# Gated heads taken in pairs, with the four values of a pair projected token-major

## The chip, the cores and the metric

The kernel runs on one core of a Trainium2 chip. The metric is the device time of one execution in microseconds (us); lower is better. The engines are named as the profile names them: PE is TensorE (PEld its weight loads), DVE is VectorE, ACT is ScalarE, POOL is GpSimd and SP is SyncE.

## The reference, cut to what matters

Two transformer blocks of 512 tokens and width 1024 are computed in float32. The change lies in the first block, where eight heads run side by side. Each head has an mLSTM part (a) and a stick-breaking part (b), and their sum is gated:

```python
p = rms_norm(x, norm_mix_g) @ w_in        # q_a k_a v_a o_a i_a f_a q_b k_b v_b g_a g_b
qk_a = silu(causal_conv(concat(q_a, k_a), conv_w))
h_a = mlstm_chunkwise(q_a, k_a, v_a, i_pre, f_pre)          # P @ v_a over s <= t, 64 wide keys, 128 wide values
y_a = sigmoid(o_a) * head_rms_norm(h_a)
y_b = stick_breaking(head_rms_norm(q_b), head_rms_norm(k_b), v_b)   # A @ v_b over s < t, 128 wide
y = sigmoid(g_a + b) * y_a + sigmoid(g_b + b) * y_b
x = x + y @ w_out
```

After it come the MLP of the first block (1024 to 4096 and back) and the second block, which the change leaves as they are.

## The kernel before, in words

**Projections.** Every projection is made of tiles of 128 output rows by 512 columns. A tile is eight steps over the width of 1024, and in each step three matmuls in the single-pass float32 format (high part by high part, low by high, high by low), 24 in all (`project`, L294). The result goes into one of two PSUM banks of `proj`, by the parity of the tile's number; a tile waits until the tile before the last has been read out (`tile_free`). Four tiles share a weight group of 2 MB. A group comes from HBM in two halves (`w_raw`, a queue on SP), ACT makes its high half (`split_hi`, L261), DVE its low half (`split_lo`, L267), and there are two slots for split groups. With `tokens=True` the activations are the stationary operand and the weights stream, so that the tile comes out with tokens on the partitions; otherwise features are on the partitions.

**A head.** Head `h` has eight tiles: 0 q_b, 1 k_b, 2 q_a and k_a together, 3 v_b (first group), 4 v_a, 5 o_a, 6 g_a, 7 g_b (second group). All are feature-major. Attention needs the values token-major, so ACT copies tiles 3 and 4 out of PSUM into `v_bT` and `v_aT`, PE turns them by eight 128x128 transposes (L1439), and ACT copies the turned ones back into `v_b` and `v_a` (L583, L584). The other small steps of a head on PE are the sums of squares of q_b and k_b (L1424, L1425), the stick scores (L1430), the gated scores (L1446), ten transposes of the stick weights `beta` (L1456), the gated sums with `decay` as the stationary operand and `v_a` streaming (L1462), four transposes of `y_tok` (L1468), and the stick sums with `v_b` (L1411).

**The order of the work is written out by hand for each engine,** with semaphores between them. On PE a head is: tiles 0, 1, 2, squares, tile 3, stick scores, tiles 4, 5, value transposes, gated scores, tile 6, `beta` transposes, gated sums, tile 7, `y_tok` transposes, stick sums; then the next head begins. So while one of the slower chains on ACT, DVE and POOL runs, PE makes a projection tile. Three such chains matter here:

- gated weights: ACT's exponential of `decay` (L581), DVE's product with the gated scores (L1000), POOL's causal mask (L449), and then the gated sums on PE;
- token norm: after the gated sums four squares on ACT (L592), small steps on DVE (L1007 to L1013), a logarithm and an exponential on ACT (L595, L597), DVE's product into `y_tok` (L1015), and then the `y_tok` transposes on PE;
- end of a head: after the stick sums five steps on DVE (L1028 to L1035), the last of which sets `head_done`. ACT's copies of the next head, POOL's broadcast of the next head's row of gates (`bc`, L439) and the output projection wait for it.

ACT has two table sets in use: one with logarithm and exponential, one with the sigmoid. A change of set is one ACT_TABLE_LOAD, four in each head. Head 0 is written out and heads 1 to 7 are a loop. The output projection (`G_OUT`, eight tiles, the last step of the first of which waits for the last `head_done`) follows at once.

Of the kernel before, what the change touches and what calls it, by code (L numbers as in the profile page):

```python
# [9 lines left out]
ALU = mybir.AluOpType  # L10
# [3 lines left out]
P = 128  # L14
# [8 lines left out]
DQK_A = 64  # L23
HD_B = 128
# [53 lines left out]
def program(nc, x_in, wall, gains, head_par, sb_gains, b_if, *rest):  # L78
    *block2_in, out = rest
    with ExitStack() as ctx:  # L80
# [41 lines left out]
        def at(name, offset, shape, dt=F32):  # L122
# [13 lines left out]
        names = "q_b k_b sq_q sq_k conv silu k_a v_bT v_aT v_b gate_o gate_a gate_b".split()  # L136
        (q_b, k_b, sq_q, sq_k, conv, silu, k_a, v_bT, v_aT, v_b, gate_o, gate_a, gate_b) = [
            at(n, (61 + 2 * i) * K, [P, SEQ]) for i, n in enumerate(names)]
        v_a = at("v_a", 87 * K, [P, TB, P + 1])
        y_tok, scl = sq_k, silu  # L140
# [272 lines left out]
        def _(pool):  # L413
# [11 lines left out]
            gp.memset(v_a[:, :, P:P + 1], 1.0).then_inc(S["consts"], 1)  # L425
# [73 lines left out]
        def _(act):  # L499
# [39 lines left out]
            with a.Fori(0, HEADS) as h:  # L539
                n = T_HEADS + 8 * h  # L540
                ga = G_HEADS + 2 * h

                a.preload_act_table_set("natural_log_exp_and_others")
                split_hi(ga + 1, 0, 0)

                for j, (raw, sq) in enumerate(((q_b, sq_q), (k_b, sq_k))):
                    a.wait_ge(S["tile_made"], n + j + 1)
                    a.wait_ge(S["head_done"], h + 1)
                    a.activation(raw[:, :], proj[:, j], ACT.Copy)
                    a.activation(sq_hi[:, j], proj[:, j], ACT.Square)  # L550
                    a.activation(sq[:, :], proj[:, j], ACT.Square).then_inc(S["tile_free"], 1)
                split_hi(ga + 1, 0, 1)

                a.wait_ge(S["tile_made"], n + 3)
# [9 lines left out]
                a.wait_ge(S["tile_made"], n + 4)  # L564
                a.activation(v_bT[:, :], proj[:, 1], ACT.Copy).then_inc(S["tile_free"], 1)
                split_hi(ga + 2, 1, 0)
# [5 lines left out]
                a.wait_ge(S["tile_made"], n + 5)  # L572
                a.activation(v_aT[:, :], proj[:, 0], ACT.Copy).then_inc(S["tile_free"], 1)

                a.activation(silu[:, :], conv[:, :], ACT.Sigmoid).then_inc(S["silu_sig"], 1)
                a.preload_act_table_set("natural_log_exp_and_others")
                split_hi(ga + 2, 1, 1)
                a.wait_ge(S["tile_made"], n + 6)
                a.activation(gate_o[:, :], proj[:, 1], ACT.Copy).then_inc(S["tile_free"], 1)
                a.wait_ge(S["arg_a"], 4 * h + 4)  # L580
                a.activation(decay[:, :], decay[:, :], ACT.Exp).then_inc(S["decay_exp"], 1)  # L581
                a.wait_ge(S["v_turned"], h + 1)
                a.activation(v_b[:, :], pa[:, 0:512], ACT.Copy).then_inc(S["v_sb"], 1)  # L583
                a.activation(v_a[:, :, 0:P], pa[:, 512:1024].rearrange("p (t n) -> p t n", t=TB), ACT.Copy).then_inc(S["v_sb"], 1)  # L584
                a.wait_ge(S["tile_made"], n + 7)
                a.activation(gate_a[:, :], proj[:, 0], ACT.Copy).then_inc(S["tile_free"], 1)
                a.wait_ge(S["a_turned_b"], h + 1)
                a.activation(aT[:, :], pa[:, 0:TRI_COLS], ACT.Copy).then_inc(S["a_b"], 1)

                a.wait_ge(S["num_made"], h + 1)  # L590
# [8 lines left out]
                a.wait_ge(S["tile_free"], n + 7)  # L599
                a.activation(gate_o[:, :], gate_o[:, :], ACT.Sigmoid).then_inc(S["gate_sig"], 1)  # L600
                a.activation(gate_a[:, :], gate_a[:, :], ACT.Sigmoid, bias=par[:, 5:6]).then_inc(S["gate_sig"], 1)
                a.wait_ge(S["tile_made"], n + 8)
                a.activation(gate_b[:, :], proj[:, 1], ACT.Sigmoid, bias=par[:, 6:7]).then_inc(S["tile_free"], 1)
# [297 lines left out]
        def _(dve):  # L901
# [4 lines left out]
            v.memset(tick[:, 2:3], 0.0).then_inc(S["pad_zero"], 1)  # L906
            def square_sum(t):
# [42 lines left out]
            with v.Fori(0, HEADS) as h:  # L950
                ga = G_HEADS + 2 * h

                v.wait_ge(S["head_done"], h + 1)
# [4 lines left out]
                split_lo(ga + 1, 0, 0)  # L958
                for j, sq in enumerate((sq_q, sq_k)):
                    v.wait_ge(S["tile_free"], T_HEADS + 8 * h + j + 1)  # L960
                    v.tensor_tensor(sq_lo[:, j], sq[:, :], sq_hi[:, j], ALU.subtract).then_inc(S["sq_lo"], 1)
                split_lo(ga + 1, 0, 1)
# [5 lines left out]
                v.wait_ge(S["par_head"], 3 * h + 3)  # L968
                v.wait_ge(S["pad_zero"], h + 2)
                v.wait_ge(S["tile_free"], T_HEADS + 8 * h + 3)  # L970
# [5 lines left out]
                split_lo(ga + 2, 1, 0)  # L976

                v.wait_ge(S["bc_landed"], 16 * h + 16)
                for i in range(TB):
                    v.tensor_scalar(decay[:, TRI[i]:TRI[i] + SEQ - P * i], bc[:, P * i:], col[:, i:i + 1], 0.0,  # L980
                                    ALU.add, ALU.min).then_inc(S["arg_a"], 1)
                v.wait_ge(S["silu_sig"], h + 1)
# [3 lines left out]
                v.tensor_copy(k_a[DQK_A:P, :], silu[0:DQK_A, :]).then_inc(S["silu_done"], 1)  # L986
                v.wait_ge(S["keep_masked"], 4 * h + 4)
# [9 lines left out]
                split_lo(ga + 2, 1, 1)  # L997
# [4 lines left out]

                v.wait_ge(S["num_sq"], 4 * h + 4)
                for i, (sign, least) in enumerate(((-1.0, floor[:, :]), (1.0, tok[:, 0]))):
# [13 lines left out]

                v.wait_ge(S["y_turned"], h + 1)
                v.wait_ge(S["gate_sig"], 2 * h + 1)  # L1020
                v.scalar_tensor_tensor(scl[:, :], pm[:, 1024:1536], par[:, 4:5], gate_o[:, :], ALU.mult, ALU.mult)\
                    .then_inc(S["y"], 1)
                v.wait_ge(S["gate_sig"], 2 * h + 2)
                v.wait_ge(S["y"], 4 * h + 1)
                v.tensor_tensor(scl[:, :], scl[:, :], gate_a[:, :], ALU.mult).then_inc(S["y"], 1)
                v.wait_ge(S["pv_b_made"], h + 1)
                v.wait_ge(S["tile_free"], T_HEADS + 8 * h + 8)
                v.tensor_tensor(gate_b[:, :], pa[:, 0:512], gate_b[:, :], ALU.mult).then_inc(S["y"], 1)  # L1028
                v.wait_ge(S["y"], 4 * h + 3)
                v.tensor_tensor(scl[:, :], scl[:, :], gate_b[:, :], ALU.add).then_inc(S["y"], 1)  # L1030
                v.wait_ge(S["y"], 4 * h + 4)
# [4 lines left out]
                    .then_inc(S["head_done"], 1)  # L1036
            v.wait_ge(S["head_done"], HEADS + 1)
# [334 lines left out]
        def _(pe):  # L1372
# [12 lines left out]
            def gate_rows():  # L1385
# [7 lines left out]
                mm.then_inc(S["a_turned"], 1)  # L1393

            def head(h, first=False):
                n = T_HEADS + 8 * h
                ga = G_HEADS + 2 * h

                def tile(j):
# [383 lines left out]
```

## Time and profile before

| | us |
|---|---|
| median of 3 runs | 1264.02 (1262.86 to 1264.53) |
| the profiled execution | 1262.79 |
| its span, first to last instruction | 1260.5 |
| PE busy in the span | 1240.2 (98%) |
| DVE busy | 694.1 (55%) |
| ACT busy | 606.6 (48%) |
| POOL busy | 47.8 (4%) |

A row of a timeline gives the start of an instruction from the start of the span, its duration, engine, line, operation, what it writes and reads, and how many neighbours were merged into it; in brackets stands how long the engine had been idle before it and what released it. Matmuls are pipelined: each lasts longer than the distance to the next, so what a matmul costs is the distance of the starts. PEclk is the clock granted to TensorE, 1.00 being 2.4 GHz.

### The profile page before, as it was taken

What the parts mean: (1) busy time and instruction counts of PE and PEld (TensorE: products, weight loads), DVE (VectorE), ACT (ScalarE), POOL (GpSimd) and SP (SyncE); (2) the same over time, 40 slices, a digit from 0 to 9 for tenths busy, and PEclk for the clock granted to TensorE, in tenths of its full rate; (3) what the DMA queues carried; (4) which work ended last, traced back from release to release, by engine and by line L of the source; (5) the groups of instructions that cost most, each with busy time, mean ns of one, the idle gap of its engine ahead of it and who ended that gap; (6) DMA issues with size and microseconds to landing.
All of it is one profiled execution on the core that took longest, in us unless ns stands there. A gap on an engine that the chain in (4) does not pass through costs nothing.

```text
span 1260.5 us, 15952 instructions
## 1 busy us (share of the span) xinstructions
PE 1240.2 (98%) x5912; PEld 1008.2 (80%) x5912; DVE 694.1 (55%) x1179; ACT 606.6 (48%) x894; POOL 47.8 (4%) x146
## 2 busy tenths in 40 slices
PE   6999999999999999999999999999999999999998
PEld 5788888888888888888888888888867777677787
DVE  6646455554645555552443433445468989666671
ACT  6745565564556563441321421335456655566820
POOL 1000000000000020000000000000000000000000
PEclk9999999999999999999999999999999999999999
DMA  6323222132322234223231322333213233535621
GB/s 219 110 75 100 75 67 87 64 100 75 100 75 67 85 125 168 68 88 113 68 132 67 100 100 100 101 108 150 76 67 110 104 119 129 201 126 166 251 67 67
DMA packets 26398, 134.48 MB, mean 107 GB/s; under 512 B 3224, under 2 KB 4312, under 8 KB 13552
## 3 DMA queue, kind: packets, MB, share of 16 engines
q1 hardware_dynamic: 16992, 107.49, 25.3%
q0 software_dynamic: 4752, 16.92, 3.9%
q10 hardware_dynamic: 4608, 9.44, 2.0%
q8 instruction: 32, 0.52, 0.2%
q14 instruction: 14, 0.11, 0.0%
HBM read 122.28 MB, written 11.55 MB: 106 GB/s over the span
## 4 chain that ended last, share of the span: by engine, by line
PE 84%; DVE 10%; ACT 3%; issue 2%; DMA 1%; ACTq 0%; DVEq 0%; SPq 0%
PE proj L294 74%; DVE idx L1271 2%; DVE w_lo L267 2%; DVE top L1267 2%; PE pm L1462 1%; PE pa L1411 1%; PE pa L1430 1%; DVE p_sb L1250 1%; PE pm L1446 1%; PE pa L1648 1%; ACT w_hi L261 1%; PE pa L1456 1%; ACT p_sb L792 1%; DVE p_sb L1261 1%; DVE idx L1164 1%
## 5 line engine op out<-in xcount | busy, mean ns | idle before, releaser
L294 PE MATMUL proj<-h_hi,w_hi 128*128 128x512 f32 (+1 forms) x976 | 385.7, 395 | 2.0 <-DVE w_lo L267 1.0
L294 PE MATMUL proj<-h_hi,w_lo 128*128 128x512 f32 (+1 forms) x976 | 377.1, 386 | 0.0
L294 PE MATMUL proj<-h_lo,w_hi 128*128 128x512 f32 (+1 forms) x976 | 376.7, 386 | 0.0
L267 DVE TENSOR_TENSOR w_lo<-w_raw,w_hi 128x2048 fp32r<-128x2048 f32 x100 | 227.9, 2290 | 89.8 <-ACT w_hi L261 88.9
L261 ACT ACTIVATE w_hi<-w_raw 128x2048 fp32r<-128x2048 f32 x100 | 189.8, 1912 | 127.0 <-PE proj L294 121.3
L294 PEld LDWEIGHTS proj<-h_hi,w_hi 128*128 128x128 f32 x976 | 183.4, 188 | 46.0 <-issue 9.9
L294 PEld LDWEIGHTS proj<-h_lo,w_hi 128*128 128x128 f32 x976 | 183.5, 188 | 38.3 <-issue 2.9
L294 PEld LDWEIGHTS proj<-h_hi,w_lo 128*128 128x128 f32 x976 | 183.3, 188 | 37.5
L294 PE MATMUL proj<-w_hi,act_hi 128*128 128x512 f32 x256 | 99.8, 390 | 0.0
L294 PE MATMUL proj<-w_lo,act_hi 128*128 128x512 f32 x256 | 99.6, 389 | 0.0
L294 PE MATMUL proj<-w_hi,act_lo 128*128 128x512 f32 x256 | 99.6, 389 | 0.0
L1097 DVE TENSOR_TENSOR x_res<-x_res,proj 128x512 f32<-128x512 f32 x32 | 21.9, 686 | 92.2 <-PE proj L294 92.2
L633 ACT ACTIVATE relu<-proj 128x512 f32<-128x512 f32 x32 | 19.2, 599 | 106.5 <-PE proj L294 106.5
L1083 DVE TENSOR_TENSOR relu_sq<-relu 128x512 f32<-128x512 f32 x32 | 22.2, 694 | 73.4 <-ACT relu L633 73.4
L294 PE MATMUL proj<-w_hi,h_hi 128*128 128x512 f32 (+1 forms) x160 | 62.2, 389 | 0.0
L294 PE MATMUL proj<-w_lo,h_hi 128*128 128x512 f32 (+1 forms) x160 | 61.9, 387 | 0.0
L294 PE MATMUL proj<-w_hi,h_lo 128*128 128x512 f32 (+1 forms) x160 | 61.7, 386 | 0.0
L294 PEld LDWEIGHTS proj<-w_hi,act_lo 128*128 128x128 f32 x256 | 48.1, 188 | 10.0
L294 PEld LDWEIGHTS proj<-w_lo,act_hi 128*128 128x128 f32 x256 | 48.1, 188 | 10.0
L294 PEld LDWEIGHTS proj<-w_hi,act_hi 128*128 128x128 f32 x256 | 48.1, 188 | 9.8
L792 ACT ACTIVATE p_sb<-p_sb,mx 128x128 f32<-128x128 f32 (+1 forms) x64 | 35.1, 550 | 31.8 <-DVE mx L1253 31.8
L294 PEld LDWEIGHTS proj<-w_hi,h_hi 128*128 128x128 f32 x160 | 30.0, 188 | 7.4 <-issue 1.5
(394 smaller groups left out, 1650.2 us busy)
## 6 DMA issues: line engine op xcount, KB each, us to landing
w_raw<-in_wall SPq DMA_DIRECT2D x100, 1024.0 KB, 5.1
gates<-gate_st ACTq DMA_DIRECT2D x24, 256.0 KB, 2.1
m_all<-gates POOLq DMA_DIRECT2D x2, 1280.0 KB, 7.5
x_res<-in_x ACTq DMA_DIRECT2D x4, 512.0 KB, 5.2
bc<-gate_rows POOLq DMA_DIRECT2D x8, 256.0 KB, 3.5
x_res<-in_x POOLq DMA_DIRECT2D x4, 512.0 KB, 4.8
x<-x_res POOLq DMA_DIRECT2D x1, 2048.0 KB, 7.4
g_all<-gates POOLq DMA_DIRECT2D x1, 2048.0 KB, 11.2
```

Source lines behind the costliest of these rows:

```text
L261: nc.scalar.activation(w_hi[:, slot, 4 * half:4 * half + 4, :], w_raw[:, half], ACT.Copy)\
L267: nc.vector.tensor_tensor(w_lo[:, slot, 4 * half:4 * half + 4, :], w_raw[:, half], w_hi[:, slot, 4 * half:4 * half + 4, :], ALU.subtract)\
L294: mm = nc.tensor.matmul(proj[:, bank, 0:cols] if tokens else proj[:, bank, toks], lhsT, rhs, start=(k == 0 and q == 0), stop=(k == kts - 1 ...
L633: a.activation(relu[:, i % 2], proj[:, i % 2], ACT.Relu).then_inc(S["tile_free"], 1)
L792: a.activation(x, x, ACT.Exp, bias=mx[:, u, i:i + 1], accum_out=row_sum[:, u, i:i + 1])\
L1083: v.tensor_tensor(relu_sq[:, i % 2], relu[:, i % 2], relu[:, i % 2], ALU.mult).then_inc(S["a_sq"], 1)
L1097: v.tensor_tensor(xx, xx, proj[:, t % 2], ALU.add).then_inc(S["tile_free"], 1)
L1164: v.scalar_tensor_tensor(idx[:, c], rel[h % 2][:, c], w_idx[:, i, h:h + 1], idx[:, c] if h else causal[:, 384 - P * i:512], ALU.mult, ALU. ...
L1250: v.tensor_tensor_reduce(p_sb[u][:, c], X[:, c], mask(i), scale(i), -3.0e38, ALU.add, ALU.max, mx[:, u, i:i + 1]).then_inc(S[f"smax{u}"], 1)
L1261: v.tensor_scalar(x, x, row_sum[:, u, i:i + 1], None, ALU.mult).then_inc(S[f"p_norm{u}"], 1)
L1267: v.max(top8[:, i - 1, :], idx[:, LOW[i]:LOW[i] + P * (i + 1)]).then_inc(S["top_max"], 1)
L1271: v.match_replace(x, top8[:, i - 1, :], x, TAKEN).then_inc(S["top_out"], 1)
```

## The change

Two heads `h = 2p` and `2p + 1` make a pair, with four weight groups and sixteen tiles: 0 q_b, 1 k_b, 2 q_a k_a, 3 o_a of the even head; 4 to 7 the values; 8 g_a and 9 g_b of the even head; 10 q_b, 11 k_b, 12 q_a k_a, 13 o_a, 14 g_a, 15 g_b of the odd head. The value group holds v_b and v_a of both heads side by side (512 columns), and its four tiles are token-major, one for each block of 128 tokens. ACT copies each of them straight into `v_b` and `v_a`, which now have room for two heads. The eight value transposes and the two buffers between are gone. The number of tiles, 64, stays.

```diff
+PAIRS = HEADS // 2
+QKA, O_A, VALUES, G_A, G_B, NEXT = (2, 12), (3, 13), 4, (8, 14), (9, 15), 16
...
+            def value_tile(n, t):
+                a.wait_ge(S["tile_made"], n + VALUES + t + 1)
+                a.activation(v_b[:, :, t], proj[:, t % 2, 0:2 * P].rearrange("p (u d) -> p u d", u=2), ACT.Copy)
+                a.activation(v_a[:, :, t, 0:P], proj[:, t % 2, 2 * P:4 * P].rearrange("p (u d) -> p u d", u=2), ACT.Copy)\
+                    .then_inc(S["tile_free"], 1)
...
-                t_.wait_ge(S["tile_free"], n + 5)
-                t_.wait_ge(S["z_sb"], 2 * h + 2)
-                for m, vT in enumerate((v_bT, v_aT)):
-                    for i in range(TB):
-                        mm = t_.transpose(pa[:, 512 * m + P * i:512 * m + P * (i + 1)], vT[:, P * i:P * (i + 1)], ident[:, :])
-                mm.then_inc(S["v_turned"], 1)
```

The order on PE for a pair; tiles 16 and 17 are q_b and k_b of the next pair and are made ahead of it. The last pair, written out after a loop over the other three, has none:

```diff
+            def pair(p, more=True):
+                n_v = T_HEADS + 16 * p + VALUES
+                for u in range(2):
+                    h = 2 * p + u
+                    if u:
+                        for j in (9, 10, 11):
+                            head_tile(p, j)
+                    head_tile(p, QKA[u])
+                    square_sums(h)
+                    head_tile(p, O_A[u])
+                    stick_scores(h)
+                    head_tile(p, G_A[1] if u else VALUES)
+                    head_tile(p, G_B[1] if u else VALUES + 1)
+                    gated_scores(h)
+                    if u == 0:
+                        head_tile(p, VALUES + 2)
+                        head_tile(p, VALUES + 3)
+                    elif more:
+                        head_tile(p, NEXT)
+                    stick_turns(h)
+                    gated_sums(h, u, n_v)
+                    if u == 0:
+                        head_tile(p, G_A[0])
+                    elif more:
+                        head_tile(p, NEXT + 1)
+                    head_turns(h, u)
+
+            head_tile(0, 0, first=True)
+            head_tile(0, 1)
+            gate_rows()
+            with t_.Fori(0, PAIRS - 1) as p:
+                pair(p)
+            pair(PAIRS - 1, more=False)
```

`gated_sums` waits for its masked weights (`p_masked`) as before and, new, for the last value tile to be read out:

```diff
+            def gated_sums(h, u, n_v):
                 t_.wait_ge(S["p_masked"], 4 * h + 4)
+                t_.wait_ge(S["tile_free"], n_v + TB)
```

On ACT the gates are no longer copied out and passed through the sigmoid later: the sigmoid reads the tile in PSUM (`gate_tile`). The order of ACT in the odd head:

```diff
+                h = 2 * p + 1
+                a.preload_act_table_set("natural_log_exp_and_others")
+                for j in range(2):
+                    qk_tile(n + 10 + j, 2 * p + 1, j)
+                conv_tile(h, n + QKA[1])
+                gate_tile(n + O_A[1], gate_o)
+                split_hi(g + 4, 1, 0)
+                sticks(h)
+                split_hi(g + 4, 1, 1)
+                a.wait_ge(S["par_head"], 3 * h + 3)
+                gate_tile(n + G_A[1], gate_a, par[:, 5:6])
+                gate_tile(n + G_B[1], gate_b, par[:, 6:7])
+                a.preload_act_table_set("natural_log_exp_and_others")
+                decays(h)
+                if more:
+                    split_hi(g + 5, 0, 0)
+                    qk_tile(n + NEXT, 2 * p + 2, 0)
+                stick_turns(h)
+                variance(h)
+                if more:
+                    qk_tile(n + NEXT + 1, 2 * p + 2, 1)
+                    split_hi(g + 5, 0, 1)
```

and in the even head: `conv_tile`, `gate_tile` of tile 3, a `split_hi`, `sticks`, value tile 0, the preload of the other table set, a `split_hi`, value tile 1, `decays`, value tiles 2 and 3, `stick_turns`, `variance`, a `split_hi`, `gate_tile` of tile 8, a `split_hi`, `gate_tile` of tile 9. DVE has the steps of before in a like order; its product of the stick sums with `gate_b` counts up `pv_read`, and the sums of squares on PE now wait for that and no more for `head_done`. `y_tok` has a place of its own and no longer shares that of `sq_k`. The columns of the weight groups are laid out on the host to match.

## Rows read from the trace of the kernel before

**Rows 1.** The page: engines, granted clock by slice, one costly group of DVE.
```profile
PE 1240.2 (98%) x5912; PEld 1008.2 (80%) x5912; DVE 694.1 (55%) x1179; ACT 606.6 (48%) x894; POOL 47.8 (4%) x146
...
PEclk9999999999999999999999999999999999999999
...
L267 DVE TENSOR_TENSOR w_lo<-w_raw,w_hi 128x2048 fp32r<-128x2048 f32 x100 | 227.9, 2290 | 89.8 <-ACT w_hi L261 88.9
```

**Rows 2.** Two stretches: length; busy (instructions) of PE, PEld, DVE, ACT, POOL; clock; DMA.
```profile
35.35:466.32 430.97, 430.97 (x2048) 351.04 (x2049) 228.15 (x315) 243.65 (x341) 29.13 (x105) 1.00 0.26 85
471.87:488.19 16.32, 16.32 (x73) 13.51 (x72) 6.76 (x15) 1.56 (x3) 0.57 (x2) 1.00 0.55 196
```

**Rows 3.** Timeline of PE in the third head, first instruction of each step.
```profile
134.96 0.47 PE L294 MATMUL proj<-h_hi,w_hi 128*128 128x512 f32 x1
...
157.74 0.27 PE L1430 MATMUL pa<-k_b,q_b 128*128 128x128 f32 x1
...
159.49 0.80 PE L294 MATMUL proj<-h_hi,w_hi 128*128 128x512 f32 x1
...
165.38 0.39 PE L294 MATMUL proj<-h_hi,w_hi 128*128 128x512 f32 x1
...
170.83 0.27 PE L1439 MATMUL pa<-ident,v_bT 128*128 128x128 f32 x1
...
171.79 0.69 PE L1446 MATMUL pm<-silu,k_a 64*128 64x512 f32 x1
...
173.28 0.50 PE L294 MATMUL proj<-h_hi,w_hi 128*128 128x512 f32 x1
...
178.88 1.25 PE L1456 MATMUL pa<-ident,beta 128*128 128x128 f32 x10
179.97 0.28 PE L1462 MATMUL pm<-v_a,decay 128*128 128x129 f32 x1
...
182.12 0.48 PE L294 MATMUL proj<-h_hi,w_hi 128*128 128x512 f32 x1
...
187.68 0.60 PE L1468 MATMUL pm<-ident,sq_k 128*128 128x128 f32 x4
...
190.19 0.47 PE L294 MATMUL proj<-h_hi,w_hi 128*128 128x512 f32 x1
```

**Rows 4.** Timeline of ACT in the same head.
```profile
171.52 1.26 ACT L581 ACTIVATE decay<-decay 128x1280 f32<-128x1280 f32 x1
...
179.07 0.60 ACT L586 ACTIVATE gate_a<-proj 128x512 f32<-128x512 f32 x1 [5.32 <-PE proj L294]
...
187.88 0.69 ACT L603 ACTIVATE gate_b<-proj,par 128x512 f32<-128x512 f32 x1 [0.51 <-PE proj L294]
188.58 1.28 ACT L543 ACT_TABLE_LOAD   x1
```

**Rows 5.** Timeline of DVE in the same head.
```profile
154.70 0.75 DVE L965 SCALAR_TENSOR_TENSOR k_b<-k_b,sbg,sq_k 128x512 f32<-128x512 f32 x1 [0.49 <-ACT sq_k L563]
...
175.05 1.49 DVE L1000 SCALAR_TENSOR_TENSOR decay<-pm,decay 128x1280 f32<-128x1280 f32 x1
...
184.84 0.69 DVE L1015 TENSOR_TENSOR sq_k<-pm,tok 128x512 f32<-128x512 f32 x1 [0.51 <-ACT tok L597]
...
192.67 0.69 DVE L1035 TENSOR_TENSOR y_lo<-silu,y_hi 128x512 f32 x1
```

**Rows 6.** Timeline of POOL in the same head.
```profile
176.60 1.03 POOL L449 TENSOR_SCALAR_AFFINE_SELECT decay<-decay 128x128 f32<-128x128 f32 x4 [10.39 <-DVE decay L1000]
```

**Rows 7.** Timeline of ACT in the second block: a tile read out in two halves.
```profile
892.08 0.38 ACT L694 ACTIVATE kv_b<-proj 128x256 f32<-128x256 f32 x1 [3.36 <-PE proj L294]
892.36 0.38 ACT L695 ACTIVATE t_k<-proj 128x256 f32<-128x256 f32 x1
```

**Rows 8.** Timeline of PE at the start: three transposes early, and three later.
```profile
8.51 0.84 PE L336 MATMUL pa<-ident,xs 128*128 128x128 f32 x3
...
13.40 0.49 PE L336 MATMUL pa<-ident,xs 128*128 128x128 f32 x3
```

More of the change, by code:

```diff
@@ L135, in program @@
         bc = at("bc", 57 * K, [P, SEQ])
[L136 to L140, printed above, removed]
+        q_b, k_b, sq_q, sq_k, conv, silu, k_a = [
+            at(n, (61 + 2 * i) * K, [P, SEQ]) for i, n in enumerate("q_b k_b sq_q sq_k conv silu k_a".split())]
+        v_b = at("v_b", 75 * K, [P, 2, TB, P])
+        gate_o, gate_a, gate_b = [at(n, (79 + 2 * i) * K, [P, SEQ]) for i, n in enumerate(("gate_o", "gate_a", "gate_b"))]
+        v_a = at("v_a", 85 * K, [P, 2, TB, P + 1])
+        y_tok, scl = at("y_tok", 59 * K, [P, SEQ]), silu
         qk_pad = at("qk_pad", 47 * K, [P, 3 + SEQ])
@@ L538, in _, with qk_tile, conv_tile @@
             a.activation(g_out[:, 1, :], g_m[:, :], ACT.Exp, scale=-1.0).then_inc(S["rows_act"], 1)
[L539 to L554, printed above, removed]
+            def qk_tile(n, heads, j):
+                raw, sq = ((q_b, sq_q), (k_b, sq_k))[j]
+                a.wait_ge(S["tile_made"], n + 1)
+                if heads is not None:
+                    a.wait_ge(S["z_made"], heads)
+                a.activation(raw[:, :], proj[:, j], ACT.Copy)
+                a.activation(sq_hi[:, j], proj[:, j], ACT.Square)
+                a.activation(sq[:, :], proj[:, j], ACT.Square).then_inc(S["tile_free"], 1)
+            def conv_tile(h, n):
+                a.wait_ge(S["tile_made"], n + 1)
                 a.wait_ge(S["head_done"], h + 1)
@@ L1393, in gate_rows, with head_tile, square_sums @@
                 mm.then_inc(S["a_turned"], 1)
[L1395 to L1399, printed above, removed]
[L1400 to L1421 removed]
+            def head_tile(p, j, first=False):
+                made(project(G_HEADS + 4 * p + j // 4, (1 + j // 4) % 2, T_HEADS + 16 * p + j, j % 2, j % 4, first=first,
+                             tokens=VALUES <= j < VALUES + TB))
+            def square_sums(h):
+                t_.wait_ge(S["pv_read"], h + 1)
                 for j in range(2):
@@ L1470, in head, with pair @@
                 t_.wait_ge(S["a_b"], h + 1)
-                weighted(pa[:, 0:512], lambda i: v_b[:, P * i:P * (i + 1)], aT).then_inc(S["pv_b_made"], 1)
-            head(0, first=True)
-            with t_.Fori(1, HEADS) as h:
-                head(h)
+                for i in range(TB):
+                    mm = t_.matmul(pa[:, P * i:SEQ], v_b[:, u, i], aT[:, TRI[i]:TRI[i] + SEQ - P * i],
+                                   start=(i == 0), stop=(i == TB - 1))
+                mm.then_inc(S["pv_b_made"], 1)
+            def pair(p, more=True):
+                n_v = T_HEADS + 16 * p + VALUES
[10 more added lines that the diff above has]
+                    head_tile(p, G_B[1] if u else VALUES + 1)
+                    gated_scores(h)
+                    if u == 0:
[3 more added lines that the diff above has]
+                        head_tile(p, NEXT)
+                    stick_turns(h)
+                    gated_sums(h, u, n_v)
[8 more added lines that the diff above has]
+            with t_.Fori(0, PAIRS - 1) as p:
+                pair(p)
+            pair(PAIRS - 1, more=False)
             t_.wait_ge(S["head_done"], HEADS)
```

192 lines of the change are left out of this document (122 added, 70 removed).

## The prediction

> **What bounds the kernel now.** I read the page first: PE is busy for 98% of the span and the granted clock stands at its upper level, 2.4 GHz, in every slice [rows 1]. Then the window over the heads: from the third tile of head 0 to the first output tile it is 430.97 us, and PE is busy in all of them, DVE in 228 and ACT in 244 [rows 2]. So here only what PE issues sets the time, and every chain of the other engines is covered by a projection tile. The timeline of one head shows the cost of each step as the distance of the starts [rows 3]: a head is 190.19 - 134.96 = 55.23 us; a tile is 165.38 to 170.83 = 5.45; after the stick scores 5.89, after the gated scores 5.60, after the gated sums 5.56, since a float32 step still drains there.
>
> **What is removed.** Eight transposes a head, 170.83 to 171.79 = 0.96 us, with the switch to the next step in them [rows 3]; eight heads make 7.7 us. From below: ten `beta` transposes take 1.09, 0.109 each, so eight alone are 0.87, or 7.0 in all [rows 3]. I take 7.7, as the gated scores will now follow a tile, and the `beta` transposes do so at no visible switch. (The Trainium skill, "TensorE: Matmul & The Clock Gate", part on PE-mode transpose, puts a 128x128 transpose at about 275 ns within a kernel; 64 of them would be an estimated 17.6 us. The rows differ: one lasts 0.27 but the next starts 0.11 later, and the start counts.)
>
> **What is turned round.** The value tiles stream weights over stationary activations instead of the reverse. The output tiles do just that: three of them fill 16.32 us, 5.44 each [rows 2]. Cost zero; it is 64 tiles before and after.
>
> **What leaves ACT.** Two copies into `v_bT` and `v_aT`, two back, and the copies of two gates a head; value tiles cost two copies of 256 columns, a pattern that shows as 0.28 from first start to second and 0.38 for the second, 0.66 for the tile [rows 7]. Table loads go from eight to six a pair. ACT was busy 244 of 431 us [rows 2]: none of this is on the path, gain zero. The load of weights stays one group per four tiles, so SP's queue keeps its pace, and it waits only for the splits.
>
> **The new order, wait by wait.** I laid a pair out with the steps of [rows 3]; u = 0 begins with tile 2 at 0.
> - Even head: tile 2 at 0, squares 5.6, tile 3 at 6.5, stick scores 11.9, tiles 4 and 5 from 13.7, gated scores 25.0, tiles 6 and 7 from 26.5, `beta` transposes 37.5, gated sums 38.6, tile 8 at 40.7, `y_tok` transposes 46.3, stick sums 46.7.
> - Odd head: tiles 9 to 12 from 48.8, squares 70.7, tile 13 at 71.6, stick scores 77.0, tiles 14, 15 from 78.8, gated scores 90.1, tile 16 from 91.6, `beta` transposes 97.2, gated sums 98.3, tile 17 at 100.4, `y_tok` transposes 106.0, stick sums 106.4, end 108.5, which is 2 x 55.23 - 1.92.
>
> Against these dates: (a) Stick scores want the normed k_b. Before, it was there at 155.45, 2.3 before their start at 157.74 [rows 3, 5]; squares and one tile stand before them as ever, so 2.3 stay. At the seam of two pairs DVE is free again 3.2 after the stick sums (192.67 + 0.69 against 190.19) plus one split of 2.29 and 0.5 of small copies, 6.0, and the first rstd comes about 7.5: free. (b) `y_tok` ends 184.84 + 0.69 = 185.53, 5.56 after the start of the sums at 179.97, and is wanted after 7.71 [rows 3, 5]: 2.15 to spare in both heads of a pair inside the loop. (c) New wait of the gated sums on value tile 3: nothing but these sums, tile 8 and the rest of the head queues behind it on PE. The tile ends with the start of the `beta` transposes; ACT begins 0.19 later (179.07 against 178.88), 0.66 of copies end at 0.85, and the sums want their start at 1.09 [rows 3, 4, 7]. It fits by about 0.2, less the semaphore and the weight load that PE pulls ahead, so 0 to 0.2 a pair, 0 to 0.8 in all; I take 0.1. (d) Gates O and the first of the even head's second group pay a table load of 1.28 beside 0.69 [rows 4]: bank free 2.2 after the tile, wanted again after 7. Free. (e) `decay` in the odd head waits for the sigmoid of tile 15 and a table load: at 93.6 its exponential ends (3.45 after tile 15, as worked out below), DVE's product ends 95.1, POOL's mask 96.2, sums due 98.3. Covered by 2.1, because tile 16 lies before them. (f) Splits: DVE's last step on `beta` ends at about 89.6 and a split of the second half follows with 2.29 [rows 1], so it is there at 91.9; PE reads it at 94.3 (half a tile into tile 16): covered by 2.4.
>
> **The last pair has no cover.** Tiles 16 and 17 were pulled ahead of head 1 and its mates, so at the end they are missing. From the start S of the last gated scores:
> - PE could begin the sums at S + 1.49 + 0.16 + 1.09 = S + 2.7 [rows 3].
> - ACT starts on tile 15 at S + 0.20, load at S + 0.90, `decay` at S + 2.19, done at S + 3.45 (0.69, 1.28 and 1.26) [rows 4]; DVE's product of 1.49 ends S + 4.97 [rows 5]; POOL starts 0.06 later and takes 1.03 [rows 6]; S + 6.1. **First wait 3.4 us.**
> - Sums 2.15; `y_tok` is there 5.56 after their start; without tile 17 PE is ready after 2.15. **Second wait 5.56 + 0.05 - 2.15 = 3.45 us.**
> - The stick sums and the tail to `head_done` follow as before: 3.2 after their end, while the output tile asks for it in its eighth step, 4.8 in: free.
>
> Together 6.85 of new idle time, once. On restart PE's first instruction is about 0.1 late, as a first tile after a step is 5.56 and not 5.45, twice 0.1.
>
> **The sum.** -7.7 + 6.85 + 0.1 + 0.2 = -0.55; with the dates laid out in a row, 3 x 108.5 and the last pair's 104.4 from 35.35, the first output tile comes at 465.3 instead of 466.32, -1.0. I take -0.8. Behind that stage everything shifts rigidly: PE is the bound there too. Made against the profiled execution, 1262.79 (span 1260.5 and 2.3 around it), this is 1262.0; the median of the runs lies 1.2 higher, so 1263.2 for the median.
>
> **The rivals.**
> - *Slower: the clock falls in the last pair.* Place: the two waits of 3.4 us with 2.2 of work between them, within 12 us of the output tiles. For it: after an idle start PE ran at half pace, three transposes taking 0.84 at 8.51 and 0.49 at 13.40, the one at the pace of 1.2 GHz and the other at that of 2.4, though the clock line shows only the upper level [rows 1, 8]. Against it: the head stretch holds no idle time at all, so this trace shows no wait of that length with a warm engine [rows 2]. Price: the low phase at the start lasted about 5 us, 8.51 to 13.40 [rows 8]. If it falls in the first wait, the sums cost 2.15 more, the closing 2.5 us twice, and up to 5 us of the output tile another 2.5: 4.6 to 7.2. In the second alone: 2.5. Net of -0.8 it gives 1265 to 1269.6, middle 1267.5. It decides once the clock falls in either wait. (The Trainium skill, "TensorE: Matmul & The Clock Gate", HAM oscillation, says that idle gaps between bursts send the clock back to half; by it this rival would be the rule and the change a loss. No row here tells.)
> - *Slower: a date inside the loop is missed,* such as (b) or (f), by a DVE that is later than laid out: four times 1 to 2 us, 1267 to 1271. Against it: the smallest of those margins is 2 us.
> - *Faster: the last pair does not wait,* the whole 7.7 stays: 1256.3. For it: PE has no idle time in any head now. Against it: the chain of S + 6.1 is made of five rows and no tile is left to cover it.
> - *It does less than it says:* the transposes cost only 0.87, or less beside the tiles' drains, 7.0 in all: 1263.9 to 1264.5, no change either.
>
> **How the numbers follow.** About 0.2%, 2.5 us, can be told from no change. Forecast with its near misses (1261.8 to 1264.5) 0.65, less than it says 0.08, clock 0.12, loop 0.08, faster 0.07. The likeliest is 1263.2. Same: forecast, less, and a small part of the clock's (one wait only), 0.73; faster than 1261.5: 0.10 with the forecast's lower edge; slower than 1266.5: 0.17. The range takes the forecast and its bounds, and half of the two slower cases: 1261.0 to 1267.8.
>
> **What would show it.** In the profile after: no line of value transposes; a pair of 108.5 us with PE wholly busy in the loop; one idle of about 3.4 us before the last gated sums, released by POOL's mask, and one of about 3.4 before the last `y_tok` transposes, released by DVE; matmuls of 0.39 after both if the clock stays up, about twice that if not. A pair over 109 us, or waits of the gated sums for ACT's value copies above 0.2 each, would prove the layout wrong.

## The result, and the profile after

| us | before | after |
|---|---|---|
| median, same chip, 12 runs each | 1264.49 (1262.72 to 1267.40) | 1267.22 (1265.26 to 1269.50) |
| the profiled execution | 1262.79 | 1269.5 |
| its span | 1260.5 | 1267.6 |

The ratio is 1.0023, interval 1.0014 to 1.0032: 2.7 us slower where 0.8 faster was forecast. The predicted range holds the time, the predicted direction is wrong.

The page of the kernel after: span, busy time of the engines, and the granted clock in 40 slices.

```profile
span 1267.6 us, 15706 instructions
...
PE 1240.3 (98%) x5848; PEld 1006.2 (79%) x5848; DVE 694.6 (55%) x1180; ACT 580.2 (46%) x871; POOL 71.3 (6%) x146
...
PEclk9999999999999989999999999999999999999999
```

64 PE instructions are gone (5912 before, [rows 1]) and PE's busy time is the same to 0.1 us: the rest must have become dearer. ACT lost 26 us and POOL gained 23, of which more below. And one slice of the clock line, the one from 444 to 475 us, is below 9. Before, none was.

The timeline of PE in the kernel after, where the heads begin and at the three seams between pairs:

```profile
36.90 0.79 PE L297 MATMUL proj<-h_hi,w_hi 128*128 128x512 f32 x1 [2.29 <-ACT sq_q L550]
...
147.18 0.47 PE L297 MATMUL proj<-h_hi,w_hi 128*128 128x512 f32 x1
...
255.98 0.47 PE L297 MATMUL proj<-h_hi,w_hi 128*128 128x512 f32 x1
...
364.82 0.47 PE L297 MATMUL proj<-h_hi,w_hi 128*128 128x512 f32 x1
```

A pair is 108.80 and 108.84 us, where 108.5 was laid out. So the loop does gain: 2 x 55.23 - 108.8 = 1.66 us a pair. Tile 2 of head 0, the first tile of the stretch, starts 1.55 later than in [rows 2], and its first matmul takes 0.79 and not 0.50, at half pace; the whole tile takes 6.99 and not 5.57. That stands ahead of every step that the change touches; e1 below has the same code there and its tile takes 5.55.

The same view, PE in the last pair from the gated scores of head 7 to the first output tile:

```profile
455.10 0.69 PE L1535 MATMUL pm<-silu,k_a 64*128 64x512 f32 x1
...
456.58 1.31 PE L1544 MATMUL pa<-ident,beta 128*128 128x128 f32 x10
461.23 4.67 PE L1553 MATMUL pm<-v_a,decay 128*128 128x129 f32 x20 [3.33 <-POOL decay L452]
469.12 0.65 PE L1560 MATMUL pm<-ident,y_tok 128*128 128x128 f32 x4 [3.23 <-DVE y_tok L1073]
469.61 4.01 PE L1564 MATMUL pa<-aT,v_b 128*128 128x512 f32 x8
473.31 0.55 PE L297 MATMUL proj<-w_hi,y_hi 128*128 128x512 f32 x1
```

Both forecast waits are there, at the forecast places and released by the forecast engines: the one before the sums by POOL's mask, the one before the turns by DVE's `y_tok`. But between them the gated sums take 469.12 - 3.23 - 461.23 = 4.66 us, not 2.15 [rows 3], and from the turns of `y_tok` to the output tile it is 4.19, not 2.51. From scores to output tile it is 18.2 us, where the layout gave 1.49 + 0.16 + 1.09 + 3.4 + 2.15 + 3.45 + 2.51 = 14.25.

The reason is in the windows of the kernel after (stretch; length; busy and count of PE, PEld, DVE, ACT, POOL; granted clock; DMA share; GB/s):

```profile
44.00:440.00 396.00, 396.00 (x1847) 321.24 (x1846) 204.45 (x283) 198.26 (x291) 46.41 (x91) 1.00 0.25 82
459.00:460.00 1.00, 0.00 (x0) 0.00 (x0) 1.00 (x1) 0.60 (x1) 0.00 (x0) 0.90 0.91 369
460.00:461.00 1.00, 0.00 (x0) 0.00 (x0) 0.08 (x1) 0.00 (x0) 0.85 (x4) 0.50 0.89 377
...
464.00:466.00 2.00, 1.90 (x9) 1.59 (x8) 0.00 (x0) 0.07 (x1) 0.00 (x0) 0.50 0.78 320
466.00:468.00 2.00, 0.00 (x0) 0.00 (x0) 0.65 (x4) 1.18 (x9) 0.00 (x0) 0.84 0.01 4
468.00:470.00 2.00, 0.88 (x5) 0.69 (x6) 0.88 (x2) 1.94 (x4) 0.00 (x0) 1.00 0.00 0
470.00:472.00 2.00, 2.00 (x4) 0.99 (x3) 1.26 (x2) 2.00 (x2) 0.00 (x0) 0.51 0.03 8
```

PE goes idle at 457.9. The clock stays at its upper level (2.4 GHz) into the slice 459 to 460, whose mean of 0.90 puts the fall to the lower one (1.2 GHz) at 459.8, within the wait; it is up again before 468, while PE is idle a second time, and falls again at about 470, with PE already at work on the stick sums. So the clock fell twice, the second time 4.1 us after the sums had ended; that each wait has its fall is argued here and shown by e1, e2 and e5. This is the first rival of the prediction. (The Trainium skill, "TensorE: Matmul & The Clock Gate", HAM oscillation, has idle gaps between bursts send the clock back to half; these windows agree.)

**A second, smaller surprise** is in the heads. The timelines of POOL and DVE in an odd head of the loop, and POOL's in an even one, kernel after:

```profile
133.67 3.10 POOL L452 TENSOR_SCALAR_AFFINE_SELECT decay<-decay 128x128 f32<-128x128 f32 x4 [9.07 <-DVE decay L1057]
...
175.85 1.02 POOL L452 TENSOR_SCALAR_AFFINE_SELECT decay<-decay 128x128 f32<-128x128 f32 x4 [7.61 <-DVE decay L1057]
```

```profile
133.84 2.29 DVE L270 TENSOR_TENSOR w_lo<-w_raw,w_hi 128x2048 fp32r<-128x2048 f32 x1 [0.23 <-ACT w_hi L264]
```

The same four masks take 3.10 us in place of 1.03 [rows 6] when DVE's split runs beside them. The longest of the 32 single masks took 2.37 us where the median is 0.29: it stood still for the length of the split, which itself took its usual 2.29. The masks of `beta` are longer too, all along, and this is where most of POOL's 23 us come from: 14.6 of them, against 6.2 from `decay`. In before DVE was idle beside them, in after it works. Single masks as least, median and longest in ns, kernel after; before, `decay` and `beta` took 1.03 and 1.02 for four in the third head:

```profile
L447 POOL TENSOR_SCALAR_AFFINE_SELECT beta<-beta x32: 492/620/1237, 56.6 to 449.9; 128x128 f32<-128x128 f32 x32
...
L452 POOL TENSOR_SCALAR_AFFINE_SELECT decay<-decay x32: 287/292/2369, 67.0 to 460.9; 128x128 f32<-128x128 f32 x32
```

On `decay` it matters. The masks end at 136.77, and PE starts the gated sums at 136.83, where they were due at about 136.77. Of the 2.1 us that I had given this chain, nothing is left. (The Trainium skill, "SBUF — State Buffer", part on its two separate sides, says that a DVE instruction with two inputs in SBUF and a GpSimd one that reads SBUF exclude each other for a whole instruction; these rows agree.)

**The account** of the head stretch, from tile 2 of head 0 to the first output tile:

| term | forecast | measured in after |
|---|---|---|
| eight sets of transposes | -7.7 | -7.1 (shown by e4) |
| two waits of the last pair | +6.85 | +6.56 |
| restart of PE, and its last matmul before an idle time | +0.2 | 2.50 - 2.15 + 2.57 - 2.51 = +0.4, at full pace (e2, e1) |
| slow clock between and behind the waits | 0 | 4.66 - 2.50 + 4.19 - 2.57 = +3.8 |
| gated sums of odd heads late, beside the value wait | +0.1 | about +0.5 |
| sum | -0.55 | +4.2 |
| the stretch itself | | 436.41 - 1.42 (slow first tile) - 430.97 = +4.0 |

The sums take 2.15 us up to the next start, but 2.50 to their own end when nothing follows them, as e2 below shows at full pace; so 0.4 of the 4.2 us by which sums and turns are longer than laid out is no matter of the clock.

With the 1.55 us of the later start and the 1.42 of the first tile, it makes the 6.99 us by which the output tile is late (473.31 against 466.32). The two spans differ by 7.1, so behind the heads all shifts rigidly, as forecast.

### The profile page after: what moved, and what is told of

Its sections match the earlier page's. It is cut to its first block, busy times and chain, and to the rows that moved or that the text cites. A ratio compares the mean times of both kernels' runs of the same rounds, so it can differ in the third digit from the quotient of the medians.

```text
span 1267.6 us, 15706 instructions
## 1 busy us (share of the span) xinstructions
PE 1240.3 (98%) x5848; PEld 1006.2 (79%) x5848; DVE 694.6 (55%) x1180; ACT 580.2 (46%) x871; POOL 71.3 (6%) x146
## 4 chain that ended last, share of the span: by engine, by line
PE 84%; DVE 10%; ACT 3%; issue 2%; DMA 1%; POOL 0%; ACTq 0%; SPq 0%; DVEq 0%
PE proj L297 73%; DVE idx L1385 2%; DVE w_lo L270 2%; PE pm L1553 2%; DVE top L1381 2%; PE pa L1564 1%; PE pa L1525 1%; DVE p_sb L1364 1%; PE pm L1535 1%; PE pa L1773 1%; ACT p_sb L841 1%; DVE p_sb L1375 1%; PE pa L1544 1%; DVE idx L1278 1%; ACT w_hi L264 1%
## 5 line engine op out<-in xcount | busy, mean ns | idle before, releaser
L297 PE MATMUL proj<-h_hi,w_hi 128*128 128x512 f32 (+1 forms) x848 | 334.0, 394 | 2.3 <-ACT sq_q L550 2.3
L297 PE MATMUL proj<-h_hi,w_lo 128*128 128x512 f32 (+1 forms) x848 | 327.5, 386 | 0.0
L297 PE MATMUL proj<-h_lo,w_hi 128*128 128x512 f32 (+1 forms) x848 | 327.2, 386 | 0.0
L297 PEld LDWEIGHTS proj<-h_hi,w_lo 128*128 128x128 f32 x848 | 159.6, 188 | 32.5
L297 PE MATMUL proj<-w_hi,h_hi 128*128 128x512 f32 (+1 forms) x288 | 114.0, 396 | 0.0
L297 PE MATMUL proj<-w_lo,h_hi 128*128 128x512 f32 (+1 forms) x288 | 111.8, 388 | 0.0
L297 PE MATMUL proj<-w_hi,h_lo 128*128 128x512 f32 (+1 forms) x288 | 111.6, 388 | 0.0
L297 PEld LDWEIGHTS proj<-w_hi,h_hi 128*128 128x128 f32 x288 | 54.1, 188 | 14.5 <-issue 3.8
L297 PEld LDWEIGHTS proj<-w_hi,h_lo 128*128 128x128 f32 x288 | 54.1, 188 | 11.4 <-issue 1.0
L297 PEld LDWEIGHTS proj<-w_lo,h_hi 128*128 128x128 f32 x288 | 54.1, 188 | 10.6
```

Of the source, the lines that this page charges most:

```text
L297: mm = nc.tensor.matmul(proj[:, bank, 0:cols] if tokens else proj[:, bank, toks], lhsT, rhs, start=(k == 0 and q == 0), stop=(k == kts - 1 ...
```

## The experiments

Three things were open: whether the clock, and not the waits alone, made the loss; what the transposes had really been worth; and where the spread of some 3 us in both kernels came from. Medians are set against runs of the kernel before on the same chip.

### e1: PE kept busy through both waits

```diff
+            def fill(n, count):
+                t_.wait_ge(S["tile_free"], n + 15)
+                for i in range(count):
+                    t_.matmul(proj[:, 0], ones_r[:, :], h_hi[:, i % KT], start=True, stop=True)
...
+                    if u and not more:
+                        fill(T_HEADS + 16 * p, 14)
                     gated_sums(h, u, n_v)
...
+                    else:
+                        fill(T_HEADS + 16 * p, 13)
                     head_turns(h, u)
```

> The changed kernel, with PE kept busy in the last pair's two waits by matmuls whose results nobody reads: 14 before the last gated sums and 13 before the last y_tok transposes, 0.227 us each, so 3.2 and 2.95 us of waits of 3.33 and 3.23. They take no time of their own. Clock theory (the waits cost 6.6 us, and 4.2 more because the granted clock falls in them): the clock stays at its upper level, the 20 gated sums last about 2.4 and not 4.67, the closing stick sums 2.1 and not 3.7, and the kernel is 4.2 us faster than the change, -1.0 to -1.5 us against the kernel before, ratio 0.999. Rival (the clock has nothing to do with it, the loss lies in the loop or at the start): no change against the changed kernel, ratio about 1.002.

Measured: 1262.95 (1261.98 to 1269.48, 12 runs) against 1264.48, ratio 0.9997 (0.9983 to 1.0011). PE in the profile of e1:

```profile
451.50 0.69 PE L1535 MATMUL pm<-silu,k_a 64*128 64x512 f32 x1
...
454.05 3.45 PE L1571 MATMUL proj<-h_hi,ones_r 128*128 128x512 f32 x14
457.64 2.50 PE L1553 MATMUL pm<-v_a,decay 128*128 128x129 f32 x20
459.89 3.22 PE L1571 MATMUL proj<-h_hi,ones_r 128*128 128x512 f32 x13
463.36 0.66 PE L1560 MATMUL pm<-ident,y_tok 128*128 128x128 f32 x4 [0.25 <-DVE y_tok L1073]
463.85 2.32 PE L1564 MATMUL pa<-aT,v_b 128*128 128x512 f32 x8
465.93 0.48 PE L297 MATMUL proj<-w_hi,y_hi 128*128 128x512 f32 x1
```

The chains take as long as before, but 27 matmuls whose result nobody reads stand in the waits. The sums then take 2.25 and not 4.66, and scores to output tile 14.4 us: the layout's 14.25 within 0.2. That is 3.8 us less than in after, for added work, and so what the slow clock costs. By the medians the kernel is 4.3 us faster than after, by the ratios to before 3.3 (0.9997 and 1.0023); the two did not run side by side. (Nine of its runs, at a clock of 0.999 or 1.0, lie up to 1264.4; the three above, 1266.7 to 1269.5 at 0.995 to 0.997, are most likely falls at the start, which e9 looks at.) The cause is the clock; the waits alone would have given the forecast, no change.

### e2 and e5: one wait only, and half of each

e2 keeps only the first 14 unread matmuls.

> The changed kernel with the 14 unread matmuls before the last gated sums alone. Clock theory: gated sums at full pace (about 2.4 us for the 20), the second wait of 3.3 us left as it is, the clock falls in it and the stick sums last 3 to 4 us; from the last gated scores to the first output tile about 15.9 us, against 18.2 in the changed kernel. Rival (one fall that follows the whole head, whatever the waits): both groups stay slow, 18.2.

e5 puts 7 before the sums and 7 before the turns.

> The changed kernel with 7 unread matmuls (1.6 us) at the head of each of the last pair's two waits, so that about 1.8 and 1.65 us of idle time are left in them. In the profiles so far the clock stayed up over waits of 1.69 us and less and fell in waits of 1.96 and more. Clock theory, by the length of the idle stretch: both groups at full pace, 2.3 for the sums and 2.1 for the stick sums, from the last gated scores to the first output tile about 14.4 us. Rival (the clock falls by the low share of work over the whole tail, so halving the idle stretches is not enough): sums or stick sums at half pace, 16 to 18 us.

Measured, one run each: e2 1265.41, e5 1261.68. PE in e2, first sums, then turns and stick sums:

```profile
458.10 2.50 PE L1553 MATMUL pm<-v_a,decay 128*128 128x129 f32 x20
463.81 1.12 PE L1560 MATMUL pm<-ident,y_tok 128*128 128x128 f32 x4 [3.21 <-DVE y_tok L1073]
464.72 4.48 PE L1564 MATMUL pa<-aT,v_b 128*128 128x512 f32 x8
```

and its windows in the second wait and behind it:

```profile
461.00:462.00 1.00, 0.00 (x0) 0.00 (x0) 0.16 (x1) 0.78 (x7) 0.00 (x0) 1.00 1.06 426
462.00:463.00 1.00, 0.00 (x0) 0.00 (x0) 0.48 (x3) 0.38 (x2) 0.00 (x0) 0.92 0.36 143
463.00:464.00 1.00, 0.19 (x1) 0.19 (x2) 0.69 (x1) 0.98 (x2) 0.00 (x0) 0.50 0.04 16
464.00:466.00 2.00, 2.00 (x6) 1.40 (x6) 0.93 (x2) 1.99 (x2) 0.00 (x0) 0.50 0.00 0
```

The second wait brings the clock down also where the first is filled, here at 462.84 by the mean of 0.92, 2.2 us after PE stopped at 460.60. The half pace reaches into the output tile, so scores to output tile is 16.9 us, 2.5 over e1. In e5 the same two places show:

```profile
457.17 2.50 PE L1553 MATMUL pm<-v_a,decay 128*128 128x129 f32 x20 [1.72 <-POOL decay L452]
459.43 1.86 PE L1571 MATMUL proj<-h_hi,ones_r 128*128 128x512 f32 x7
462.89 0.66 PE L1560 MATMUL pm<-ident,y_tok 128*128 128x128 f32 x4 [1.60 <-DVE y_tok L1073]
```

with the sums at 2.26 and 14.4 us from scores to output tile. Two idle times of 1.7 and 1.6 us, with dense matmuls ahead of them, left the clock up; in this one run it was enough to break the waits, not to fill them.

### e3: real work in the waits

Instead of unread matmuls, the last pair gets another order: tile 15 after the gated scores; on ACT its sigmoid at the very end, so that `decay` comes first; stick sums before the `y_tok` turns; and the last split of DVE waits for POOL's mask.

```diff
                     gated_scores(h)
+                    if u and not more:
+                        head_tile(p, G_B[1])
...
-                gate_tile(n + G_B[1], gate_b, par[:, 6:7])
+                if more:
+                    gate_tile(n + G_B[1], gate_b, par[:, 6:7])
                 a.preload_act_table_set("natural_log_exp_and_others")
...
+                if not more:
+                    v.wait_ge(S["p_masked"], 4 * h + 4)
+                    split_lo(g + 4, 1, 1)
...
-                    head_turns(h, u)
+                    head_turns(h, u, last=u == 1 and not more)
```

> The changed kernel with another order in the last head only: tile 15 after the gated scores and not before, the exponential of decay before the sigmoid of tile 15, the stick sums before the y_tok transposes, DVE's last split after the mask. Same work. Worked out from the steps: a wait of about 0.4 us before the gated scores, none before the gated sums, about 1.3 before the y_tok transposes; from the end of tile 14 to the first output tile 14.8 us, against 23.8 in the changed kernel. Clock theory: no fall in the last head, 9 us faster than the changed kernel, about -5.5 us against the kernel before, ratio 0.9957. If only the waits and not the clock count, 5 us faster than the changed kernel, ratio about 0.998.

Measured: 1258.74 (1258.52 to 1260.41, 6 runs), ratio 0.9955 (0.994 to 0.997). The end of the heads in e3, PE:

```profile
449.98 0.66 PE L1542 MATMUL pm<-silu,k_a 64*128 64x512 f32 x1 [0.23 <-DVE k_a L1043]
...
458.13 2.40 PE L1560 MATMUL pm<-v_a,decay 128*128 128x129 f32 x20
460.36 2.32 PE L1577 MATMUL pa<-aT,v_b 128*128 128x512 f32 x8
463.75 0.65 PE L1569 MATMUL pm<-ident,y_tok 128*128 128x128 f32 x4 [1.07 <-DVE y_tok L1076]
464.16 0.47 PE L297 MATMUL proj<-w_hi,y_hi 128*128 128x512 f32 x1
```

No wait before the sums, 1.07 before the turns, everything at full pace: 14.2 us with a tile of 5.6 inside. The head stretch, less 1.33 of a slow first tile, is 425.8, or 5.2 less than before. So what the change gained in the loop it had lost at its end.

### e4: what the transposes were worth

The kernel before without its value transposes. ACT copies the values unturned, so that the attention sums are of other numbers.

```diff
-                a.wait_ge(S["v_turned"], h + 1)
-                a.activation(v_b[:, :], pa[:, 0:512], ACT.Copy).then_inc(S["v_sb"], 1)
+                a.wait_ge(S["tile_free"], n + 6)
+                a.activation(v_b[:, :], v_bT[:, :], ACT.Copy).then_inc(S["v_sb"], 1)
...
-                for m, vT in enumerate((v_bT, v_aT)):
-                    for i in range(TB):
-                        mm = t_.transpose(pa[:, 512 * m + P * i:512 * m + P * (i + 1)], vT[:, P * i:P * (i + 1)], ident[:, :])
-                mm.then_inc(S["v_turned"], 1)
```

> The kernel before with the value transposes left out (the values are copied as they are, so the attention sums are of other numbers) and nothing else moved. It measures what the removal is worth where every tile stays in its place: -7.7 us by the step of the transposes (0.96 each head), -7.0 if 0.09 of it is a switch that the gated scores then pay (the changed kernel shows the scores 0.09 later after a tile); ratio 0.9939 to 0.9945. Rival (PE was not the bound, a chain of other engines takes over): less than 4 us.

Measured: 1257.72 (1254.85 to 1261.04, 6 runs), ratio 0.9943 (0.9924 to 0.9963). The windows of e4, the slow first tile's start and the whole stretch:

```profile
36.00:37.00 1.00, 0.35 (x1) 0.35 (x2) 1.00 (x1) 1.00 (x4) 0.00 (x0) 0.50 0.56 180
...
36.65:463.35 426.70, 426.70 (x1985) 345.68 (x1985) 227.11 (x312) 244.18 (x341) 29.13 (x105) 0.99 0.26 86
```

The head stretch is 426.70, and less the 2.86 of its slow first tile 423.84: 7.1 under before, 0.89 a head. In after the two tiles ahead of the gated scores take 11.42 us and not 11.33: the switch to another kind of step, 0.09, is now paid there. It had been inside the 0.96 of the transposes and did not go with them.

### e6: the split moved off the mask

```diff
-                    split_lo(g + 5, 0, 0)
                     v.wait_ge(S["a_done"], h + 1)
                     square_low(n + NEXT, 0)
+                    split_lo(g + 5, 0, 0)
```

> The changed kernel, with DVE's first split of the value group in the odd head moved behind the square of tile 16, so that it no longer runs beside POOL's mask of decay. In the changed kernel that mask takes 3.10 us in the odd heads of the loop beside the split and 1.02 in the last head, where no split runs beside it, and the gated sums start 0.1 to 0.15 late. Theory (the two get in each other's way): mask 1.0 to 1.1 us in the loop, beta transposes and gated sums of the odd head 1.09 and 2.15 as in the even one, a pair 108.6 and not 108.8. Rival (the odd head's mask is slow by its own data or place): 3.1 us as before.

Measured, one run: 1265.78. POOL in the odd head of e6:

```profile
131.17 1.03 POOL L452 TENSOR_SCALAR_AFFINE_SELECT decay<-decay 128x128 f32<-128x128 f32 x4 [9.06 <-DVE decay L1057]
```

The mask is back at 1.03, and `beta` turns and sums of odd heads take 1.09 + 2.15, not 1.15 + 2.25. The last pair is as in after: waits of 3.33 and 3.22, 0.4 for their ends, and 3.2 us of slow clock. Its head stretch is 433.88, +2.9 over before, where -7.1 + 6.55 + 0.4 + 3.2 makes +3.05. The split beside the mask cost about 0.5 us in all, which one run alone could not have told; the steps of the timeline do.

### e7 and e8: together, and with a steady start

e7 is e3 and e6 in one.

> The last head in the new order and the split moved, both together: the sum of the two, about 6 us faster than the kernel before, ratio 0.995 (0.994 to 0.9965). If the split's move brings nothing, as the new order alone, 0.9955.

Measured: 1259.47 (1256.60 to 1261.46, 6 runs), ratio 0.9958 (0.9943 to 0.9973): no better than e3, with a spread of 5 us. Its runs at a mean clock of 1.0 are at 1256.6, those at 0.996 or 0.997 at 1260.2 to 1261.5. So another dip was hiding what the order gave. It is the one in front of head 0, where PE waits for the weights and for the first copies. e8 adds eight unread matmuls there:

```diff
             t_.wait_ge(S["w_lo_done"], 2)
+            t_.wait_ge(S["norm_lo"], 1)
+            for k in range(3):
+                t_.matmul(proj[:, 0], h_hi[:, 0, 0:P], h_hi[:, 0, :], start=True, stop=True)
...
                 mm.then_inc(S["a_turned"], 1)
+                for k in range(5):
+                    t_.matmul(pa[:, 0:512], ones_r[:, :], h_hi[:, k, :], start=True, stop=True)
```

> As the one with the new order of the last head and the moved split, and with unread matmuls in two waits ahead of the heads: 3 after the first low part of the input norm, 5 after the small transposes of the gate rows. In some executions of both kernels the clock falls there after waits of 1.96 to 2.47 us, and the third tile of head 0 then starts 1.3 to 1.6 us later and takes 6.9 to 8.4 us and not 5.57, 3 us or more in all; in others it stays up. Theory: with waits kept below 1.7 us it stays up in every execution, so the spread of the runs narrows from about 5 us to 2 or less and the median falls by 1 to 2 us below the kernel without them, ratio 0.994. Rival (the spread comes from elsewhere, such as the transfers at the start): same spread and median, or 0.5 us slower from the matmuls.

Measured: 1256.82 (1256.45 to 1257.16, 5 runs), ratio 0.9942 (0.993 to 0.9955), clock 1.0 in every run. The spread is 0.7 us. e8 beats both kernels, before by 7.3 and after, which did not run beside it, by some 10 us. Windows of e8 over the start and over the last pair (the clock column shows 1.00 also over the first transposes, which run at half pace as in [rows 8]; from 15.8 on the matmuls last 0.39 to 0.47):

```profile
8.00:36.00 28.00, 25.98 (x123) 21.79 (x123) 20.74 (x25) 20.57 (x31) 4.66 (x8) 1.00 0.53 181
446.00:462.00 16.00, 14.71 (x81) 11.76 (x81) 10.85 (x15) 8.56 (x17) 4.75 (x11) 1.00 0.53 196
```

### e9, e10 and e11: the same start under before, after and e4

The eight unread matmuls at the start are meant to take the dip there out of the comparison: e9 is before with them, e10 after, e11 is e4 (values unturned).

> The kernel before, nothing changed in the heads, with the same 8 unread matmuls in the two waits ahead of them as in the kernel with the kept start. A base line without the fall of the clock at the start. Theory: spread below 1.5 us and a median of about 1262, 2 below the kernel before (ratio 0.998 to 0.999), since the start of the heads is all that varies. Rival (the narrow spread belonged to the new order of the last head): 4 us of spread as before.

> The changed kernel with the same 8 matmuls at the start. Against the base line with the kept start it is +4.0 us by the steps of the two profiles (6.6 of waits, 4.2 of slow clock, 0.5 of late masks, less 7.1 of transposes: 4.2), about 1266, clock below 1 in every run, since the waits of the last pair are in every run. If the clock fell in that tail only now and then, the runs would part into two groups some 4 us from each other.

> The kernel before without its value transposes (values copied as they are, so the sums are of other numbers) and with the same 8 matmuls at the start. Against the base line: -7.1 us (0.89 a head), about 1255; -7.7 if the switch of 0.09 were no price. The clock stays up in all runs.

| kernel | median us (runs) | ratio to before | mean clock of the runs |
|---|---|---|---|
| e9 | 1262.68 (11) | 0.9993 (0.9984 to 1.0002) | 1.0, one 0.999 |
| e10 | 1265.85 (11) | 1.0023 (1.0014 to 1.0032) | 0.994 to 0.997 |
| e11 | 1255.96 (5) | 0.9941 (0.9928 to 0.9955) | 1.0, one 0.999 |

Ten of e9's 11 runs lie within 0.8 us, where before's own 21 lie within 4.2: 1261.8 to 1263.4 at a clock of 1.0, 1264.1 to 1264.6 at 0.999, 1265.2 to 1266.0 at 0.997. The spread of the kernel before is therefore for the most part its start. e11 is 6.7 under e9, 0.84 a head, near e4's 0.89. e10 is 3.2 over e9, less than the 4 expected, and its clock is down in every run. Its last pair in the trace:

```profile
461.21 3.98 PE L1558 MATMUL pm<-v_a,decay 128*128 128x129 f32 x20 [3.33 <-POOL decay L452]
468.40 1.12 PE L1565 MATMUL pm<-ident,y_tok 128*128 128x128 f32 x4 [3.22 <-DVE y_tok L1073]
469.31 3.24 PE L1569 MATMUL pa<-aT,v_b 128*128 128x512 f32 x8
472.31 0.47 PE L297 MATMUL proj<-w_hi,y_hi 128*128 128x512 f32 x1
```

The sums take 3.97 and turns to output tile 3.91: 2.8 us of slow clock, against 3.8 in after and 3.2 in e6. The low phases end at different points of the same work. -7.1 + 6.55 + 0.4 + 2.8 + 0.5 is +3.15, and its head stretch (38.26 to 472.31) is 3.1 over before's. So the account closes in three executions with three sizes of the clock's term. But its start was not cured in every run: they still spread over 3.8 us, six at 1265.2 to 1265.9 and five at 1267.1 to 1269.0. The profiled one, 1268.47, is of the second group; an idle time of 2.12 us is left at its start, with matmuls at half pace behind it.

## Why the prediction was wrong

- **What bounds the kernel** was right: PE alone. Its view also hid the point. "The head stretch holds no idle time at all" was used as a reason against the clock's fall, while it only meant that the trace had nothing to say on what idle time does.
- **What is removed** was mis-sized by 0.6: 7.1 and not 7.7. I chose the distance of 0.96 with its switch over the lower bound of 0.87 because tile to `beta` turns shows no visible switch; tile to gated scores does, 0.09.
- **What is turned round and what leaves ACT** were right at zero: ACT is 26 us less busy and nothing follows from it.
- **Waits (a) to (d) and (f)** held; of (c) nothing shows, as even heads keep their 1.09 and 2.16. **(e) was wrong in its working,** though it cost only 0.5: the mask was taken at 1.03 beside any work of DVE. It took 3.10, the cover of 2.1 was gone, and the sums began 0.06 late.
- **The last pair's waits** were right to 0.1 and 0.2 us: 3.33 and 3.23 for 3.4 and 3.45. The second is the shorter because the sums end 2.50 after their start and not 2.15.
- **The step that failed is "The sum".** It lets PE go on at full pace after two waits of 3.4 us: the clock has no term in it, and "How the numbers follow" gave the rival with the clock a chance of 0.12. The runs put +3.8 us there: 18.2 us from scores to output tile in after, 14.4 in e1. To judge by the mean clocks, 0.993 to 0.996 in the 12 runs of after and 0.994 to 0.997 in the 11 of e10, it fell every time; a dip at the start alone gives 0.997 in before too, so e10 against the 1.0 of e9 says more. What spoke for the rival was two rows of this trace at half pace after an idle start; what spoke against it was only silence. An unknown with a price of 5 us beside a forecast of -0.8 decides the sign, and should have had the larger chance.
- **The rival itself** had the mechanism right and a price of 4.6 to 7.2 where 3.8 came. Its times do not follow from its prices: 1263.2 plus 2.5 to 7.2 is 1265.7 to 1270.4, with a middle of 1268, and not 1265 to 1269.6. That its 1267.5 lies 0.3 off is therefore in part luck, and so is the time inside the range: the kernel before was also 0.5 us slower here than in the runs shown.
- **Faster, the last pair does not wait,** did not come, yet e3 shows that it was one reordering away.

What stays open: which idle times bring the clock down. In e6 one of 3.13 us at the start left it up, and so did one of 1.61 before the first tile of head 0. In e7 one of 1.48 at that same place was followed by a fall at 36.8, five matmuls into the tile, which took 7.16 us. Length alone does not decide it, and no run here took it apart. That both falls of the last pair come from the waits is shown by e1, e2 and e5.

## What to carry to other kernels

When a schedule takes the cover away from a chain, price the wait twice: its length, and the pace of what PE does behind it; here the second was more than half of the first, and cheap work in the wait, even unread matmuls, bought it back. A reordering that gains in a loop must be laid out for its last pass too, where nothing is left to pull ahead. When executions of one kernel spread by more than what you want to see, look for a dip of the clock outside the change and steady it in both kernels before comparing.

## What the runs showed of the hardware that was not expected

- The clock fell within the wait, 1.9 us after PE stopped in after and 2.2 in e2, rose during the next idle time, and then fell once more with PE at work. A wait of 3.2 to 3.3 us cost another 1.3 to 2.5 us behind it (after, e2, e6 and e10).
- A split of DVE with both inputs in SBUF stops POOL's masks for its whole length: 0.29 us became 2.37, while DVE lost nothing. In after and e3 four masks of `beta` take 2.84 us beside other work of DVE, a product, two copies and a scan, and 1.02 in before beside none; which of these stretches them was not taken apart.
- Two idle times of 1.7 us with 7 dense matmuls ahead of each left the clock up in e5, one run.
